# The first norm's modulation made on TensorE instead of VectorE, in a hybrid diffusion step on one core

## What is computed

```python
silu_ctx = jax.nn.silu(c_ctx)[None, :]
silu_c = jax.nn.silu(c)
ada_ctx = silu_ctx @ w_ada[l] + b_ada[l]          # context tokens; ada_lat = silu_c @ w_ada[l] + b_ada[l] for latent ones
s0, sc0, g0, s1, sc1, g1, s2, sc2, g2 = [m[:, None, :] for m in jnp.split(ada, 9, axis=-1)]
n = rmsnorm(h, P['norm_g'][l, 0]) * (1 + sc0) + s0   # rmsnorm: x * rsqrt(mean(x * x) + 1e-6) * g
h = h + 0.5 * g0 * swiglu(n, P['w_ffn_up'][l, 0], P['w_ffn_down'][l, 0])
```

## Time and profile before

| | us |
|---|---|
| median of 3 executions (lowest, highest) | 3374.37 (3373.1, 3385.32) |
| the profiled execution's own time | 3377.15 |
| its span in the profile | 3375.3 |
| PE busy in the span | 3153.0 |
| DVE busy | 1762.5 |
| ACT busy | 988.0 |
| transfers | 412.31 MB, mean 122 GB/s |

### The profile page before, as it was taken

The page is one execution under the profiler, slowest core; times in us unless marked ns, Lnnn a source line. Parts: engine busy times, 40 slices in busy tenths (PEclk is TensorE's granted clock), DMA queues, the critical chain, the costliest instruction groups (busy, mean ns, idle before and its releaser), DMA issues.

```text
span 3375.3 us, 48537 instructions
## 1 busy us (share of the span) xinstructions
PE 3153.0 (93%) x20832; PEld 3074.4 (91%) x20832; DVE 1762.5 (52%) x2924; ACT 988.0 (29%) x1502; POOL 76.7 (2%) x114
## 2 busy tenths in 40 slices
PE   2999999887999899999999999998889989999998
PEld 1999999776899899999999999997679889999998
DVE  7546565645555555343465565663455546543334
ACT  2312123323444333121242121332134433422222
POOL 0000000120000000000000000000000000000000
PEclk9999999988999999999999999998889999999999
DMA  5333333345212523232223333350721234322222
GB/s 234 119 119 150 138 134 155 121 152 213 85 70 90 207 95 119 88 113 88 103 104 120 131 149 137 114 209 26 271 78 68 81 141 152 113 100 75 76 76 69
DMA packets 71110, 412.31 MB, mean 122 GB/s; under 512 B 8240, under 2 KB 10608, under 8 KB 40432
## 3 DMA queue, kind: packets, MB, share of 16 engines
q1 hardware_dynamic: 56448, 312.50, 25.2%
q0 software_dynamic: 9312, 54.53, 4.2%
q10 hardware_dynamic: 5136, 42.18, 3.1%
HBM read 355.01 MB, written 54.17 MB: 121 GB/s over the span
## 4 chain that ended last, share of the span: by engine, by line
PE 80%; DVE 10%; ACT 4%; issue 3%; DMA 2%; POOL 0%; DVEq 0%; ACTq 0%; SPq 0%; POOLq 0%
PE tile_psum L502 36%; PE tile_psum L509 19%; PE tile_psum L792 5%; PE misc_psum L717 3%; PE tile_psum L463 3%; PE misc_psum L428 3%; PE tile_psum L428 2%; PE tile_psum L796 2%; DVE wlo L1416 1%; PE tile_psum L468 1%; PE tile_psum L654 1%; ACT whi L1014 1%; DMA raw<-in_w_mix 1%; PE tile_psum L843 1%; DVE h L1560 1%
## 5 line engine op out<-in xcount | busy, mean ns | idle before, releaser
L502 PE MATMUL tile_psum<-n_hi,whi 128*128 128x320 f32 x3264 | 744.9, 309 | 3.5 <-DVE n_lo L1485 3.3
L502 PE MATMUL tile_psum<-n_lo,whi 128*128 128x320 f32 x3264 | 742.7, 308 | 0.0
L502 PEld LDWEIGHTS tile_psum<-n_hi,whi 128*128 128x128 f32 x3264 | 546.3, 188 | 6.1 <-DVE n_lo L1485 3.1
L502 PEld LDWEIGHTS tile_psum<-n_lo,whi 128*128 128x128 f32 x3264 | 546.9, 188 | 0.0
L1416 DVE TENSOR_TENSOR wlo<-raw,whi 128x2048 fp32r<-128x2048 f32 (+2 forms) x196 | 430.7, 2198 | 199.7 <-ACT whi L1014 197.9
L509 PE MATMUL tile_psum<-n_hi,wlo 128*128 128x320 f32 x3264 | 512.2, 308 | 0.0
L1014 ACT ACTIVATE whi<-raw 128x2048 fp32r<-128x2048 f32 (+2 forms) x202 | 370.4, 1835 | 404.3 <-DMA raw<-in_w_up 197.0
L509 PEld LDWEIGHTS tile_psum<-n_hi,wlo 128*128 128x128 f32 x3264 | 486.9, 188 | 0.0
L502 PE MATMUL tile_psum<-x_hi,whi 128*128 128x320 f32 x1408 | 320.8, 308 | 0.0
L502 PE MATMUL tile_psum<-x_lo,whi 128*128 128x320 f32 x1408 | 320.2, 308 | 0.0
L1615 DVE TENSOR_TENSOR hidden<-gate_act,tile_psum 128x320 f32<-128x320 f32 x176 | 85.6, 487 | 386.1 <-ACT gate_act L1103 385.7
(11 more groups left out here) (279 smaller groups left out, 3901.1 us busy)
## 6 DMA issues: line engine op xcount, KB each, us to landing
raw<-in_w_up SPq DMA_DIRECT2D x88, 1024.0 KB, 4.8
w_ada<-in_w_ada SPq DMA_DIRECT2D x128, 512.0 KB, 5.6
raw<-in_w_down SPq DMA_DIRECT2D x32, 1024.0 KB, 4.8
raw<-in_w_gate SPq DMA_DIRECT2D x24, 1024.0 KB, 4.7
g_keep<-gate_out POOLq DMA_DIRECT2D x48, 320.0 KB, 2.5
gates<-g_keep POOLq DMA_DIRECT2D x16, 960.0 KB, 7.1
whi<-table_keep SPq DMA_DIRECT2D x14, 1024.0 KB, 4.8
wlo<-table_keep SPq DMA_DIRECT2D x14, 1024.0 KB, 7.2
```

Source lines behind the costliest of these rows:

```text
L502: pe.matmul(tps[:, t.s, m, 0:TH], blk(p, m * n + k)[0], (hi, lo)[b][:, k, tok], start=k == 0 and b == 0, stop=False)
```

## The change

Both the work and its place at the start are changed.

- A second copy of the first 16 tiles is laid out on the host by input rows (`w_first`): in each tile a block k has 128 inputs on the partitions and 128 outputs along the row. PE multiplies each block with two columns, the silu of the latent and of the context vector (`ccs`, loaded by a small transfer of 128 x 16, `c_cols`, and put through one activation), and adds up over k. That is 8 matmuls for each tile with a result of 128 x 2, 16 tiles in one PSUM tile. All operands are plain f32, and the result is two columns wide.
- The order of the tiles is `ADA_FIRST`: shift and scale of block 0, then of block 1, and so on. Fifteen have a buffer of their own; the sixteenth waits for the first to be read.
- DVE adds the bias to all 16 tiles at once and makes the norm's scale in one more operation; the 32 products and sums of DVE for them are gone.
- The squares: ACT writes all eight blocks to eight buffers with no wait between them. PE sums them over blocks and partitions itself, 2 x 3 x 8 matmuls with two columns of ones, in place of DVE's eight additions and PE's six matmuls. These stand on PE ahead of the modulation's.
- The loads: the columns, x and the constants are issued first. The broadcast vectors, the small tables and the parameters are issued by ACT after it has seen the last of the 16 tiles arrive. Silu of the broadcast vectors, keeping them, and the split of the small tables come on ACT after the first norm's first half of tokens, ahead of the first gate. SP no longer waits for `c_kept` ahead of panel 0 but ahead of panel 4.
- DVE splits panel 0 between k = 3 and k = 4 of the first norm and panel 1 after k = 7; before, both came ahead of k = 0. ACT rounds panel 0 ahead of k = 0 and panel 1 between k = 3 and k = 4.

The diff, without the parts that only pass the new arguments on:

```diff
--- before.py
+++ after.py
@@ -93,6 +93,7 @@
 ADA_EARLY = 16
+ADA_FIRST = [8 * part + k for k in range(KT) for part in range(2)]
 ADA_PLAN = [[0, 0, 2, 2, 1, 1, 1, 1] + [1] * 4 + [2] * 8 + [2, 2, 1, 1] + [2] * 6 + [1, 1, 0, 0],
@@ -216,6 +217,7 @@
             ("low_rms", [P, 16], F32), ("low_inv_rms", [P, 16], F32), ("inv_l1", [P, 8], F32))
+        ccs = lrs
         X0 = at
@@ -226,8 +228,9 @@
         (early,), _ = place(X0, ("w_ada_early", [P, 10, D], F32))
-
-        (smraw,), _ = place(N0, ("small_raw", [P, NSM], F32))
+        (sq8, early2), _ = place(N0, ("x_squares", [P, KT, T], F32), ("w_ada_early2", [P, 5, D], F32))
+
+        (smraw,), _ = place(W0, ("small_raw", [P, NSM], F32))
@@ -303,13 +306,18 @@
+        def first_tile(n):
+
+            return early[:, n % 15, :] if n % 15 < 10 else early2[:, n - 10, :]
+
         def smat(ap, at, n=P):
...
         hi_ready, lo_dve, lo_pool = sem("panel_hi_ready"), sem("panel_lo_dve"), sem("panel_lo_pool")
-        early_in = [sem(f"ada_early_in{k}") for k in range(10)]
+        early_in, first_used = [sem(f"ada_early_in{k}") for k in range(ADA_EARLY)], sem("ada_first_used")
+        cols_in, cols_ready, x_squared = sem("c_cols_in"), sem("c_cols_ready"), sem("x_squared")
         ada_in, ada_used = [sem(f"ada_in{k}") for k in range(2)], sem("ada_used")
@@ -575,8 +583,24 @@
             pe.wait_ge(consts_in, due(consts_in, 16))
-            token_sums(0)
-            token_sums(1)
+            pe.wait_ge(x_squared, KT)
+            for j in range(2):
+                norms_open[j] = m = taken(slots.misc())
+                for c, (a, _) in enumerate(TOKEN_COLS):
+                    for k in range(KT):
+                        ins = pe.matmul(mps[:, m.s, 0, 2 * c:2 * c + 2], sq8[:, k, j * TH + a:j * TH + a + P], ones[:, 0:2],
+                                        start=k == 0, stop=k == KT - 1)
+                ins.then_inc(sums_done, 1)
+            pe.wait_ge(cols_ready, due(cols_ready))
+            t = taken(slots.tile())
+            for n, tile_ in enumerate(ADA_FIRST):
+                pe.wait_ge(early_in[n], 16)
+                for k in range(KT):
+                    ins = pe.matmul(tps[:, t.s, 0, 2 * tile_:2 * tile_ + 2], first_tile(n)[:, k * P:(k + 1) * P],
+                                    ccs[:, 2 * k:2 * k + 2], start=k == 0, stop=k == KT - 1)
+                if n == 0:
+                    ins.then_inc(first_used, 1)
+            ins.then_inc(t.done, 1)
             spread(0)
@@ -878,7 +902,7 @@
             due = Due()
-            at, tiles_in = [0], [0]
+            at, tiles_in = [0], [ADA_EARLY]
@@ -887,13 +911,8 @@
                     tiles_in[0] += 1
-                    if t < ADA_EARLY:
-                        if t >= 10:
-                            sp.wait_ge(ada_used, t - 9)
-                        sp.dma_start(early[:, t % 10, :], w_ada[t]).then_inc(early_in[t % 10], 16)
-                    else:
-                        sp.wait_ge(ada_used, t - 1)
-                        sp.dma_start(adaw[:, t % 2, :], w_ada[t]).then_inc(ada_in[t % 2], 16)
+                    sp.wait_ge(ada_used, t - 1 if t > ADA_EARLY else t)
+                    sp.dma_start(adaw[:, t % 2, :], w_ada[t]).then_inc(ada_in[t % 2], 16)
@@ -917,6 +936,8 @@
                     for i in range(n):
+                        if (l, f, c, i) == (0, 0, 0, 4):
+                            sp.wait_ge(c_kept, 16)
                         load(w_up[at_up + i])
@@ -927,8 +948,10 @@
-            ada_load(ADA_EARLY)
-            sp.wait_ge(c_kept, 16)
+            for n in range(ADA_EARLY):
+                if n == 15:
+                    sp.wait_ge(first_used, 1)
+                sp.dma_start(first_tile(n), w_first[n]).then_inc(early_in[n], 16)
             for l in range(DEPTH):
@@ -1062,7 +1085,8 @@
                 act.wait_ge(t.free, t.free_at)
-                act.wait_ge(sq_used, due.now(sq_used))
+                if due.now(sq_used):
+                    act.wait_ge(sq_used, due.now(sq_used))
                 for m in range(2):
@@ -1118,32 +1142,36 @@
+            act.dma_start(ccs[:, :], c_cols).then_inc(cols_in, 16)
+            act.dma_start(h[:, :, :], x).then_inc(x_in, 16)
+            act.dma_start(cs_t[:, :], cst_in).then_inc(consts_in, 16)
+            act.wait_ge(cols_in, due(cols_in, 16))
+            act.activation(ccs[:, :], ccs[:, :], ACT.Silu).then_inc(cols_ready, 1)
+            act.wait_ge(x_in, due(x_in, 16))
+            for m in range(KT):
+                act.activation(sq8[:, m, :], h[:, m, :], ACT.Square).then_inc(x_squared, 1)
+            act.wait_ge(consts_in, due(consts_in, 16))
+            token_root(0)
+            token_root(1)
+            act.wait_ge(early_in[ADA_EARLY - 1], 16)
             act.dma_start(cb[:, :, :], cvec.partition_broadcast(P)).then_inc(c_in, 16)
-            act.dma_start(cs_t[:, :], cst_in).then_inc(consts_in, 16)
-            act.dma_start(h[:, :, :], x).then_inc(x_in, 16)
             act.dma_start(smraw[:, :], small).then_inc(small_in, 16)
             act.dma_start(pr[:, :], par[0]).then_inc(par_in, 16)
+            round_panel()
+            slots.tile()
+            norm_hi(0, 0, 0, range(4))
+            round_panel()
+            norm_hi(0, 0, 0, range(4, KT))
             act.wait_ge(c_in, due(c_in, 16))
...
             act.dma_start(c_keep, cb[:, :, :]).then_inc(c_kept, 16)
-            act.wait_ge(x_in, due(x_in, 16))
-            for m in range(KT):
-                if m:
-                    act.wait_ge(sq_used, due(sq_used))
-                square(m)
-            due(sq_used)
             act.wait_ge(small_in, due(small_in, 16))
...
             act.dma_start(sm_keep[1], sml[:, :].bitcast(F32)).then_inc(small_kept, 16)
-            round_panel()
-            token_root(0)
-            token_root(1)
-            round_panel()
-            norm_hi(0, 0, 0, range(KT))
             for l in range(DEPTH):
@@ -1404,7 +1432,7 @@
             slots = Slots(due)
-            at, tiles_done, made = [0], [0], [0]
+            at, tiles_done, made = [0], [ADA_EARLY], [ADA_EARLY]
@@ -1503,13 +1531,12 @@
                     tiles_done[0] += 1
-                    if t < ADA_EARLY:
-                        w, arrived = early[:, t % 10, :], early_in[t % 10]
+                    w, arrived = adaw[:, t % 2, :], ada_in[t % 2]
+                    dve.wait_ge(arrived, due(arrived, 16))
+                    if t == ADA_EARLY:
+                        dve.wait_ge(silu_out, due(silu_out))
                     else:
-                        w, arrived = adaw[:, t % 2, :], ada_in[t % 2]
-                    dve.wait_ge(arrived, due(arrived, 16))
-                    if t:
-                        dve.wait_ge(ada_half, t)
+                        dve.wait_ge(ada_half, t - ADA_EARLY)
                     dve.scalar_tensor_tensor(out=junk, in0=w, scalar=1.0, in1=cb[:, 0, :], op0=ALU.mult, op1=ALU.mult,
@@ -1634,23 +1661,23 @@
                 dve.sem_inc(f, 1)
-            own(dve.memset(acc[:, :], 0.0))
-            dve.wait_ge(silu_out, due(silu_out))
-            dve.wait_ge(consts_in, due(consts_in, 16))
-            ada_step(6)
-            for m in range(KT):
-                add_square()
-                ada_step(1)
-            dve.sem_inc(sum_ready, 1)
-            dve.sem_inc(sum_ready, 1)
-            ada_step(ADA_EARLY - 6 - KT)
+            m0, m1 = open_norm(0), open_norm(1)
+            t = tile()
+            b_first = cst("b_ada")[:, 0:ADA_EARLY].unsqueeze(2).broadcast_to([P, ADA_EARLY, 2])
+            dve.tensor_tensor(ada[:, 0:ADA_EARLY, :], tps[:, t.s, 0, 0:2 * ADA_EARLY].rearrange("p (a b) -> p a b", b=2), b_first, ALU.add)\
+                .then_inc(t.free, 1)
+            dve.wait_ge(t.free, t.free_at)
+            first_g = cst("norm_g")[:, 0:8].unsqueeze(2).broadcast_to([P, 8, 2])
+            own(dve.scalar_tensor_tensor(out=gm[:, 0:8, :], in0=ada[:, 8:16, :], scalar=1.0, in1=first_g, op0=ALU.add, op1=ALU.mult))
+            for _ in range(ADA_EARLY):
+                dve.sem_inc(ada_used, 1)
+            normalise(0, 0, 0, m0, range(4))
+            split_panel()
+            normalise(0, 0, 0, m0, range(4, KT))
+            split_panel()
             dve.wait_ge(small_hi, due(small_hi))
...
             dve.wait_ge(small_split, due(small_split))
-            split_panel()
-            m0, m1 = open_norm(0), open_norm(1)
-            split_panel()
-            normalise(0, 0, 0, m0, range(KT))
             for l in range(DEPTH):
@@ -2041,6 +2068,7 @@
     w_ada = inp["w_ada"].reshape(DEPTH, D, ADA_TILES, P).transpose(0, 2, 3, 1).reshape(DEPTH * ADA_TILES, P, D)
+    w_first = inp["w_ada"][0].reshape(KT, P, ADA_TILES, P).transpose(2, 1, 0, 3)[ADA_FIRST].reshape(ADA_EARLY, P, D)
     up = inp["w_ffn_up"].reshape(DEPTH, 2, KT, P, 2, HT, P)
```

(2 more changed lines are left out.)

4 lines of the change are left out of this document (2 added, 2 removed).

## The result

| | us |
|---|---|
| changed kernel, median of 4 executions (lowest, highest) | 3414.74 (3411.64, 3421.89) |
| kernel before, beside it, median of 4 | 3377.45 (3373.1, 3385.32) |
| ratio, with its 95% interval | 1.0111 [1.0084, 1.0138] |
| the profiled execution's own time, and its span | 3412.72, 3410.9 |

The changed kernel is slower by 1.1%, which is 28 to 47 us; the forecast was 28.5 us slower, 3403 us, with a range of 3395 to 3414. The direction and the mechanism of the start held; the median lies 11.7 us above the forecast and 0.7 us above the range.

The account below looks back on a forecast made before the run. PE was taken to be bound from its first panel on, so a later first pair moves the end: 24.0 + 3.1 + 1.0 + 0.4 = 28.5 us slower, forecast 3403 us, range 3395 to 3414.

Parts of the forecast that it names:

- PE is bound from the first pair on: From its first panel PE is busy without a gap, so a later start moves the end by as much.
- The stream: PE's 352 narrow passes ahead of the first panel, 0.213 us each: 20.5 us of sums and 54.6 of tiles, from 18.4.
- x moved ahead: At the start, x is loaded ahead of the broadcast vectors and lands at 12.0 to 13.1 us, taken as 12.5.
- The hole: First pair: splitting panel 0 between k = 3 and k = 4 costs 3.1 us, and a later clock rise 1.0.
- needs about the same for one k, so it has nothing stored up: First pair: PE takes about DVE's 0.89 us per k, so the split of panel 0 costs it 3.1 us.
- No load held PE: Start: loads lie beside the stream; a rival had tiles or their buffers hold PE, with no way seen to it.
- The rival of the rising clock: Clock rises in the 352-pass stream, 40.7 us against 75.1, a net 7.3 us faster: 3367 us; chance 0.10.
- The rival of the late start: Start: x lands no sooner than now, +6.1 us; 3407 to 3413 us; chance 0.08 together with the held gate.
- the held gate: First gate: the ACT tail at its bound, +3.6 us; chance 0.08 together with the late start.
- Behind the norm ACT now has, ahead of the first gate: About 6 us of ACT work delays the first gate, mostly covered by 9.4 us of PE work: 0.4 us, bounds 0 and 4.
- The other 128 modulation tiles and everything from the second pair on are as before: Everything from the second pair on is unchanged, only shifted; no term for it in the sum.
- the base: Time of the kernel before that the 28.5 us was added to: 3374.37 us, a median of three.

Follow-up runs that it names:

- delay29: Kernel before plus 148 unused narrow f32 passes on PE ahead of the first pair: 3405.98 us, ratio 1.0081; repeated, 3411.48 us, 1.0085.
- delay34: Kernel before plus 170 unused narrow f32 passes on PE ahead of the first pair: 3420.46 us, ratio 1.0114.
- wide2: Changed kernel plus unused 512-column f32 matmuls, eight ahead of the modulation's stream and two behind each of the first 15 tiles: 3426.49 us, one execution.
- inputs_only: Kernel before with the change's two new inputs passed and a few bytes of each read at the very end: 3384.30 us, ratio 1.0007.
- cover: Changed kernel with both panels' rounding and splits, silu, its keeping and the tables' split put ahead of the norm: 3412.51 us, ratio 1.0084.
- dve_sums: Changed kernel with DVE adding the squares again, PE keeping 12 of the 96 passes of sums: 3394.63 us, ratio 1.0039.
- after_plus5: Changed kernel plus 30 narrow passes on PE behind its spread of the norm: 3411.88 us, ratio 1.0095.
- after_plus10: Changed kernel plus 52 narrow passes on PE behind its spread of the norm: 3416.15 us, ratio 1.0108.
- tiles_wide: Changed kernel with tiles first, squares summed by DVE, panel splits ahead of the norm, one wide matmul per tile: 3408.20 us, ratio 1.0073.

## Why the prediction was right, and where it missed

**Right, by its steps.** PE is bound from the first pair on: delay29 and delay34 show it. The stream costs 352 x 0.213 us: measured 75.2 us for 75.1, without a gap, at 1.2 GHz to its end. x moved ahead lands in 10.8 us for a forecast 11.3, and a square takes 0.64 us for 0.74. The stream so starts 1.2 us early; 0.6 of it is lost again. Of that, 0.4 us lie behind the stream, where DVE's sixteen increments of a semaphore, which I had left out, stand ahead of the norm (the chain has DVE's first product at 94.43, with the stream's end at 92.46: 2.0 us for a forecast 1.6). The hole is where it was forecast, and 0.7 us smaller with its clock. On DVE it is nearly the size forecast; but PE, at 1.07 us for one k where DVE took 0.89, was already 0.9 us behind DVE at k = 3, and lost only 2.0 us to it (from 99.72 to 102.83, less one step), not 3.1. The sentence that PE "needs about the same for one k, so it has nothing stored up" had taken the pace of the kernel before, where the clock rose in the middle of that pair. No load held PE.

**The rival of the rising clock** was priced about right: wide2 shows that its pitch exists, 0.106 us for a priced 0.111, but its condition did not come: 75 us of records without a gap left the clock at 1.2 GHz. The Trainium skill, in "TensorE: Matmul & The Clock Gate", section "Part 1: The HAM clock gate", says that sustained matmul activity releases the throttle. Read as busy time, that is contradicted here (0.213 us a pass over 352 passes); read as a matter of what the matmuls are, it agrees with wide2. The rival of the late start did not come; its other half, the held gate, came with 2.5 us of its bound of 4.

**The step that failed**, in the sum of the start, is "Behind the norm ACT now has, ahead of the first gate ... I take **0.4 us**, bounds 0 and 4". It measured 2.5 us. The parts were right: table load 1.28, silu 1.93, high part 1.07, low part 1.24, three issues 1.1 and short waits, 6.9 us from 104.76 to the gate at 111.66, for some 6 in the forecast. The cover was wrong. I had 9.4 us of PE's work over it; but the tail began at 104.76 and pair (0, 0) ended at 108.95, so 4.2 us were covered. And what waits is more than the gate's own reader: behind the gate stand the rounding and the split of the next panel and then the norm of the second half of the tokens, which kept its distance of 5.6 us from the gate and had no slack left against PE. The first pass, 0.6 us early, and the hole, 0.7 us smaller, hid over half of that miss. So the whole start came to 29.4 us for 28.5, closer than its terms were, and that is luck.

**What carried the time out of the range** is not the start but two other steps. One is "The other 128 modulation tiles and everything from the second pair on are as before", a term put at nothing and given no width. In the first pair of traces it measured 6.2 us (span less milestone 2807.0 for 2800.8); the cause stays open. The work behind the milestone took 2800.8 and 2803.8 us in two traces of the kernel before, 2806.4 in inputs_only, 2807.0, 2815.4 and 2809.2 in three of the changed kernel, 2810.9 and 2809.0 in two of delay29, 2802.6 in cover, 2801.1 in dve_sums. It differs between traces of one kernel by up to 8.4 us. The other step is the base, 3374.37 us from three executions. Added to the 3381 us that the kernel before takes over 9 to 19, the forecast's 28.5 would have given 3409.5, and the measured start 3410.4.

**What stays open.** The changed kernel's ratio (1.0100 to 1.0111) lies some 5 us above that of a delay with the same milestone (1.0081, 1.0085). Of the explanations put on record, the new inputs' place is not supported by inputs_only (2.4 us, at most 5). A simple effect of how late the first block ends is not supported: after_plus5 shares the changed kernel's milestone and measured 1.0095, delay34 and after_plus10 share a later one (607.3, 607.0) and measured 1.0114 and 1.0108. A property of the changed kernel's own code behind the start is not supported either, since dve_sums (13.2 us over the kernel before, milestone 14.1 later) and cover (28.4, 24.5) sit on both sides of a plain sum. All these differences are within what the intervals allow, so whether there are 5 us to explain at all is not settled.

One quantity on record goes with much of it: each execution's mean granted clock. Of the 19 executions of the kernel before beside the first runs, the fastest, 3374.10 us, had 0.976 and the slowest, 3392.47, had 0.970. Over all 56 of it beside the experiments the time falls by 2.4 us for each 0.001. The twelve executions of the changed kernel have a mean of 0.9732 and the eight of the two delay29 runs 0.9749. By that slope this is an estimated 4 of the 7 us between their mean times, and delay34, the slowest for its milestone, is also low, at 0.9725. Whether the change lowers the clock behind the start, or these executions just had more low stretches, no run tells.

## What to carry to other kernels

A plain f32 matmul with a two-column result is not cheap for being narrow: its twelve passes took 2.69 us where twelve of up to 128 columns took 2.82. And 75 us of such passes, at 0.213 us each, did not bring the faster clock; so take their pitch from a stretch of the same kind, not from the engine's best. Work moved whole from a busy engine to an idle one may only move the wait: with all of the modulation on PE the start was at best 3 us sooner than with all on DVE, and half on each brought it 23 us sooner and the time 20 us down. When a tail is moved ahead of a wait, follow the whole queue behind it, on every engine that waits there; and take the base from as many runs as the claim needs.

## What the hardware showed that was not expected

- TensorE stayed at 1.2 GHz through 75.2 us of two-column f32 passes with no gap in the records. Behind eight f32 matmuls of 512 columns, and with two more behind each 16 narrow passes, the same passes ran at 0.106 us, 2.4 GHz, to the end of the stream; with one for each 16 and none ahead, they ran at 0.213 to the end.
- A pass of a plain f32 matmul of 512 columns took 0.45 us at 2.4 GHz (wide2) and 0.93 us at 1.2 GHz (tiles_wide: 1.85 us from 16.16 to 18.01 for two), while a two-column pass took 0.106 and 0.213.
- The granted clock reads 1.00 in the changed kernel's trace from its start, also where the pitch is that of 1.2 GHz (0.213 us a pass from 17 to 92 us, 1.07 us a step at 97).
- The times of one kernel went with the mean granted clock of the execution: 2.4 us for each 0.001 over 56 executions of the kernel before, from 0.970 to 0.977.
